# A two-layer hybrid transformer step on one core: late expert rows combined by matmul, final norm tile by tile, z kept in chunk order

## The reference, cut to what matters

```python
def moe(h, router_w, router_b, w_gate, w_up, w_down):
    ...
    gates = jnp.sum(jax.nn.one_hot(idx, N_EXPERTS, dtype=jnp.float32) * w[..., None], axis=1)
    a = jnp.einsum("td,edf->tef", h, w_gate)
    u = jnp.einsum("td,edf->tef", h, w_up)
    z = jax.nn.silu(a) * u * gates[:, :, None].astype(h.dtype)
    return jnp.einsum("tef,efd->td", z, w_down)
...
    x = x + gate1 * mixed
    h2 = rmsnorm(x, norm2_g) * (1 + scale2) + shift2
    x = x + gate2 * moe(h2, ...)
...
    y_prompt = rmsnorm(xp, final_norm_g)
    y_sample = rmsnorm(xs, final_norm_g)
```

## Time and profile before

| | us |
|---|---|
| median of 3 runs | 1341.26 |
| lowest, highest | 1334.2, 1343.4 |
| the profiled execution | 1344.76 |
| its span, first to last instruction | 1343.1 |
| PE busy, DVE busy, ACT busy, POOL busy | 1170.7, 525.6, 371.5, 249.6 |
| layer 0's expert loop, from 387.6 to 661.0; PE's granted clock in it | 273, 0.98 |
| layer 1's expert loop, from 1032.5 to 1306.0 | 273 |

### The profile page before, as it was taken

The page is one execution under the profiler, slowest core; times in us unless marked ns, Lnnn a source line. Parts: engine busy times, 40 slices in busy tenths (PEclk is TensorE's granted clock), DMA queues, the critical chain, the costliest instruction groups (busy, mean ns, idle before and its releaser), DMA issues.

```text
span 1343.1 us, 19689 instructions
## 1 busy us (share of the span) xinstructions
PE 1170.7 (87%) x7740; PEld 540.9 (40%) x7740; DVE 525.6 (39%) x1276; ACT 371.5 (28%) x730; POOL 249.6 (19%) x361
## 2 busy tenths in 40 slices
PE   2899899789969999999629989988896999999980
PEld 0555555354423333333225655555443333333320
DVE  1274666733422111111154747575145111111125
ACT  2123344331312222222121424452222222222221
POOL 1221274220020111110020324440202011111000
PEclk9899889789879999999959997996996999999995
DMA  9738321555769999999380312064733999999924
GB/s 364 258 125 124 65 95 67 213 200 226 317 232 379 382 382 389 400 393 377 113 301 0 134 63 83 12 222 167 300 117 149 346 396 390 391 389 384 391 113 161
DMA packets 51488, 322.71 MB, mean 240 GB/s; under 512 B 8329, under 2 KB 8777, under 8 KB 32080
## 3 DMA queue, kind: packets, MB, share of 16 engines
q1 hardware_dynamic: 37552, 286.87, 55.3%
q0 software_dynamic: 12576, 30.03, 8.4%
q10 hardware_dynamic: 1280, 4.72, 0.9%
HBM read 315.53 MB, written 22.73 MB: 252 GB/s over the span
## 4 chain that ended last, share of the span: by engine, by line
PE 74%; DVE 14%; DMA 7%; issue 2%; ACT 2%; SPq 0%; DVEq 0%; POOLq 0%; ACTq 0%
PE ps L1835 38%; PE ps L1476 18%; PE ps L1724 6%; PE ps L1824 3%; DMA ring<-ada_w 3%; DVE attT L1103 3%; DVE dbuf L1082 2%; PE ps L1487 2%; PE ps L1510 2%; PE ps L1647 1%; PE ps L1618 1%; DMA ring<-w_out 1%; DVE small L1208 1%; DVE dbuf L1078 1%; DMA expert_rows<-big,lst 1%
## 5 line engine op out<-in xcount | busy, mean ns | idle before, releaser
L1835 PE MATMUL ps<-ring,dbuf 128*32 128x512 f32 x3072 | 390.2, 598 | 3.0 <-DVE dbuf L1395 1.6
L1835 PE MATMUL ps<-extra,dbuf 128*32 128x512 f32 x1536 | 198.4, 596 | 0.0
L1835 PEld LDWEIGHTS ps<-ring,dbuf 128*32 128x32 f32 x3072 | 108.6, 111 | 212.9 <-issue 207.4
L1476 PE MATMUL ps<-ring,extra 128*128 128x512 f32 (+1 forms) x384 | 149.8, 550 | 0.0
L1476 PE MATMUL ps<-extra,ring 128*128 128x384 f32 (+1 forms) x384 | 127.8, 481 | 7.6 <-ACT extra L763 5.1
L685 POOL DMA_INDIRECT expert_rows<-big,lst x32 | 30.0, 939 | 468.6 <-DVE big L1416 446.5
L1835 PEld LDWEIGHTS ps<-extra,dbuf 128*32 128x32 f32 x1536 | 56.1, 110 | 121.1 <-issue 120.9
L1476 PEld LDWEIGHTS ps<-ring,extra 128*128 128x128 f32 x384 | 74.0, 194 | 69.7 <-issue 66.2
L1476 PEld LDWEIGHTS ps<-extra,ring 128*128 128x128 f32 x384 | 75.7, 207 | 54.8 <-issue 12.7
L1395 DVE COPY dbuf<-ps 128x384 f32<-128x384 f32 x32 | 17.8, 558 | 200.5 <-PE ps L1824 200.4
L1724 PE MATMUL ps<-ring,extra 128*128 128x512 f32 x192 | 87.5, 612 | 7.6 <-DMA ring<-w_out 6.4
(11 more groups left out here) (281 smaller groups left out, 1393.2 us busy)
## 6 DMA issues: line engine op xcount, KB each, us to landing
ring<-moe_w_up SPq DMA_DIRECT2D x30, 2048.0 KB, 14.1
ring<-ada_w SPq DMA_DIRECT2D x24, 2048.0 KB, 8.9
ring<-moe_w_gate SPq DMA_DIRECT2D x24, 2048.0 KB, 14.0
extra<-moe_w_down SPq DMA_DIRECT2D x22, 2048.0 KB, 14.4
ring<-w_in SPq DMA_DIRECT2D x12, 2048.0 KB, 11.6
ring<-moe_w_down SPq DMA_DIRECT2D x10, 2048.0 KB, 18.5
extra<-moe_w_gate SPq DMA_DIRECT2D x8, 2048.0 KB, 14.8
ring<-w_out SPq DMA_DIRECT2D x4, 2048.0 KB, 9.8
```

Of the source, the lines that this page charges most:

```text
L1476: ins = pe.matmul(out, a, b, start=(n == 0), stop=(n == len(pairs) - 1))
L1835: return pe.matmul(p[QT * g:QT * (g + 1), :], a, w, start=start, stop=stop, tile_position=(0, QT * g))
```

## The change

1. **Routing stretch.** Of the four `AHEAD` blocks in layer 0, the first is multiplied between the two halves of the logits, the second behind `hidden_back(2)`, the last two behind the lists (before: two, one and one, with the first two ahead of `hidden_tile(2)`). `modulation` on DVE moves behind the overflow table. SP holds the weights from the fourth expert block on until the first gather has landed. Layer 1 uses the slot order of layer 0.
2. **Overflow.** Its count is published ahead of the lists (`s_nov`); each engine reads it and branches before the expert loop, in both layers. Code of the loop itself is otherwise the same.
3. **Returned rows.** The last two experts (`LATE`) are not scattered. POOL, having zeroed two buffers during expert 4, gathers the rows of the first 14 experts by six indirect DMAs (two for each tile, rows of the last two left at zero), starting when scatter 13 has landed. DVE prepares 0/1 matrices (`late`) from the lists, and PE adds the last two experts' rows by matmul into PSUM (`cm`, 12 matmuls a layer); `completed` on DVE multiplies by the gate and adds. POOL sums the third tile. `expert_rows` is written once at the start from the inputs.
4. **Final norm.** Gain loaded early, one DVE instruction a tile for scale and gain, `normalize` laid between the sums, a store a tile.
5. **z.** ACT reads PSUM in order and writes in chunk order (512 B steps), DVE reads its PSUM part every fourth column; `zb` is contiguous for PE's four transposes.

```diff
@@ engine SP
+            def overflow_weights(l):
+                o_ = ov[l]
+                sp.wait_ge(s_nov, l + 1)
+                n_ov = sp.value_load(ovt[0:1, 0:1], min_val=0, max_val=MAXOV)
+                with sp.If(n_ov > 0):
...
                     elif kind == "expert":
+                        if j == 3:
+                            overflow_weights(l)
+                            sp.wait_ge(d_g[0], 16 * (NE // 2 * l + 1))
...
-            sp.dma_start(y_prompt[0], xn[:, 0, :]).then_inc(d_y, 16)
-            sp.dma_start(y_sample[0].rearrange("(t p) d -> p t d", p=P), xn[:, 1:3, :]).then_inc(d_y, 16)
+            for t in range(NT):
+                sp.wait_ge(s_y, t + 1)
+                sp.dma_start(y_sample[0, (t - 1) * P:t * P] if t else y_prompt[0], xn[:, t, :]).then_inc(d_y, 16)
@@ engine POOL
+                    if e == EXP_PER_BODY:
...
+                        for k in range(2):
+                            step(pool.memset(yr[k], 0.0))
...
+                    if 0 < e <= NE - LATE:
...
+                pool.wait_ge(s_late, l + 1)
                 for t in range(NT):
-                    pool.dma_start(yr[:, t, :, :], yrow[2 * t * P:2 * (t + 1) * P].rearrange("(p k) d -> p k d", k=2)).then_inc(d_yr[t], 16)
+                    for k in range(2):
+                        pool.indirect_dma_start(yr[k][:, t, :], None, yrow, bass.IndirectOffsetOnAxis(yidx[:, NT * k + t:NT * k + t + 1], 0),
+                                                bounds_check=2 * T - 1, oob_is_err=False).then_inc(d_yr[t], 16)
+                if l == L - 1:
+                    pool.dma_start(fin, final_norm_g.partition_broadcast(P)).then_inc(d_fin, 16)
+                pool.wait_ge(d_yr[2], 32 * (l + 1))
+                y = yr[0][:, 2, :]
+                step(pool.tensor_tensor(y, y, yr[1][:, 2, :], ALU.add))
+                step(pool.tensor_tensor(y, y, gate[:, 1, :], ALU.mult))
+                pool.tensor_tensor(x[:, 2, :], x[:, 2, :], y, ALU.add).then_inc(s_sum2, 1)
@@ engine ACT
-                        act.activation(sS[0:CAP], p[0:CAP], ACT.Silu)
-                        release(act, act.activation(sU[2 * QT:CAP], p[CAP:P], ACT.Copy), ("a", l), e)
+                        act.activation(by_chunk(sS)[0:CAP], in_rows(p)[0:CAP], ACT.Silu)
+                        release(act, act.activation(by_chunk(sU)[2 * QT:CAP], in_rows(p)[CAP:P], ACT.Copy), ("a", l), e)
@@ engine DVE, routing
+                p = ready(dve, ("cnt", l))
+                release(dve, dve.tensor_copy(cnt, p[:, 0:NE]), ("cnt", l))
...
+                dve.tensor_copy(ovt[0:1, 0:1], pin[0:1, NE - 1:NE]).then_inc(s_nov, 1)
                 p = ready(dve, ("lst", l))
...
+                step(dve.tensor_tensor(late[0:CAP].rearrange("p j t c -> p (j t) c"), places[0:CAP].unsqueeze(1).broadcast_to([CAP, LATE * NT, P]),
+                                       tokf[0:CAP].rearrange("p j t -> p (j t)").unsqueeze(2).broadcast_to([CAP, LATE * NT, P]), ALU.is_equal))
@@ engine DVE, end of the layer
+                summed(0)
+                expert(NBODY, 0, last=True, next_=False)
+                summed(1)
+                completed(0)
+                completed(1)
+                normalize(2 * l + 2, 0)
+                dve.wait_ge(s_sum2, l + 1)
+                completed(2)
+                normalize(2 * l + 2, 1)
+                normalize(2 * l + 2, 2)
@@ engine PE
-                for blk in AHEAD[l][0:2]:
-                    mod_rows(*blk)
                 hidden_tile(2)
...
-                        turn("zt", e - 1, [zb_by_f[0:CAP, f, :] for f in range(FC)])
+                        turn("zt", e - 1, [zb[0:CAP, f * P:(f + 1) * P] for f in range(FC)])
...
+                for t in range(NT):
+                    halves = [begin(pe, ("cm", l, t, b)) for b in range(2)]
+                    for j in range(LATE):
...
+                            ins = pe.matmul(halves[b], late[0:CAP, j, t, :], ybuf[0:CAP, j, b * 512:(b + 1) * 512], start=(j == 0), stop=(j == LATE - 1))
```

More of the change, by code:

```diff
@@ L173, in place_jobs @@
             uses[b] += NE
+        for job in [("cm", l, t, b) for t in range(NT) for b in range(2)]:
+            b = n % MOD_BANK
+            uses[b] += 1
+            place[job] = (b, uses[b])
+            n += 1
     return place
@@ L257, in by_row @@
             return v.rearrange("p (q a k) -> p q k a", q=4, k=KC)
-        yr = carve(big, 0, NT, 2, D)
+        yr = [carve(buf, 0, NT, D) for buf in (big, bbuf)]
+        late = carve(bbuf, NT * D, LATE, NT, P)
+        fin = ring[:, SLOTS - 1, 0:D]
         junk = carve(big, 2 * NT * D, D)
@@ L966, in expert @@
                         release(act, act.activation(ybuf[2 * QT:CAP, (es - 1) % 2, 512:1024], p[CAP:P], ACT.Copy), ("dn0", l), e - 1)
+                o_ = ov[l]
+                act.wait_ge(s_nov, l + 1)
+                n_ov = act.value_load(ovt[0:1, 0:1], min_val=0, max_val=MAXOV)
+                with act.If(n_ov > 0):
+                    with act.Fori(0, n_ov) as r:
+                        act.wait_ge(o_["tensor"], 4 * r + 2)
+                        act.activation(sS[0:CAP], ps[0:CAP, 2, :], ACT.Silu).then_inc(o_["scalar"], 1)
+                        act.wait_ge(o_["stored"], 16 * r + 16)
                 turned_out(0, 0)
@@ L1416, in expert @@
                         release(dve, dve.tensor_tensor(half, half, p[0:2 * QT], ALU.add), ("dn1", l), e - 1)
-                turned_out(0, 0)
-                for e in range(EXP_PER_BODY):
-                    expert(0, e, first=(e == 0))
-                with dve.Fori(1, NBODY - 1) as i:
-                    for e in range(EXP_PER_BODY):
-                        expert(i, e)
-                for e in range(EXP_PER_BODY):
-                    expert(NBODY - 1, e, next_=(e < EXP_PER_BODY - 1))
-                expert(NBODY, 0, last=True, next_=False)
                 o_ = ov[l]
+                dve.wait_ge(s_nov, l + 1)
                 n_ov = dve.value_load(ovt[0:1, 0:1], min_val=0, max_val=MAXOV)
@@ L1924, in _ @@
+                for t in range(NT):
+                    halves = [begin(pe, ("cm", l, t, b)) for b in range(2)]
+                    for j in range(LATE):
+                        if t == 0:
+                            for kind in ("dn0", "dn1"):
+                                moved(pe, (kind, l), NE - LATE + j)
                         for b in range(2):
-                            ins = matmuls(ps[0:CAP, 5 + b, :], [(zTg[:, f, :], wd[:, f, b * 512:(b + 1) * 512]) for f in range(FC)])
-                        ins.then_inc(o_["tensor"], 1)
```

236 lines of the change are left out of this document (136 added, 100 removed).

## The result

The changed kernel takes 1327.4 us (median of 8 runs, 1325.0 to 1334.9) beside 1339.0 for the kernel before on the same chip: ratio 0.9926, 95% interval 0.9905 to 0.9946. That is 11.6 us less, where the forecast had 33.6 on the profiled time and some 28 on the median, and its range, 1299 to 1325, ends where the measured times begin. The profiled execution took 1326.6, its span is 1324.6.

A forecast was written before the change was run, and what follows sets the result against it. The prediction took the loop as bound by PE at full clock; its terms, -12.9 -13.0 -5.9 -1.2 +1.4 -2 = -33.6 on the profiled 1344.76, gave 1311.2, stated as 1311 us, range 1299 to 1325.

The forecast's parts named there:

- End of layer 0 and 1: From the last expert to layer 1's transposes, and to the kernel's end: 12.9 and 13.0 us less.
- Tile 1: three of 1.24: At the layer's end, DVE's three sums of tile 1 behind the last expert take 1.24 us each, to 666.2.
- hidden by 6 us: At the layer's end, POOL's sum of tile 2 takes 6.9 us from 661, done at 668, hidden by 6 us.
- Half clock for the combination: Rival at the layer ends: combination tiles take 6.9 us each, gain 3.6 in place of 12.9, total 1330; chance 0.13.
- The six gathers then cost POOL what the gather of layer 1 does: At the end of layer 0, each gather costs POOL 1.04 us to issue, some 0.3 between; one lands after 3.85.
- z: Expert loop: contiguous transposes of zb save 0.1 us in each of 32 experts, weight loads up to 8; taken as -2.
- An expert's period of 16.8 and not over 16.9: Sign in the expert loop: one expert takes 16.8 us and not over 16.9.
- the 2.04 from which they would count: Rival in the loop: ACT's strided copies pace it from 2.04 us each; 1345 and more if 2.6; chance 0.04.
- The held weights: Rival: SP's late fourth block starves the loop, PE waiting in experts 1 to 3, some 8 us, 1319; chance 0.06.
- Routing, layer 0: Routing stretch of layer 0: gate matmuls at 381.7 in place of 387.60, -5.9; their fuller clock another -1.2.
- Routing, layer 1: Routing stretch of layer 1: DVE's added instructions and a load make the copy 1.4 us later (0.7 to 3).
- the rival of loads and branches: Ahead of the loop, register loads and taken branches cost 3 us more in each layer, total 1317; chance 0.11.

The follow-up runs named there:

- e6: The changed kernel with all sums of rows on DVE, tile 1's ahead of the last expert, none on POOL: 1329.3 us, ratio 0.9925.
- e8: The kernel before with six more gathers of hidden rows by POOL behind expert 13's scatter, into unread buffers, both layers: 1345.9 us, one run.
- e9: The kernel before with six plain loads of 96 hidden rows in place of the gathers of e8: 1339.6 us, one run.
- e11: e10 with plain loads of the returned rows in place of the six gathers, each layer with its own zero-filled rows: 1316.6 us, ratio 0.9838.
- e2: The changed kernel with z strided as in the kernel before: 1329.6 us, ratio 0.9933.
- e3: The changed kernel with SP issuing expert blocks before routing, without its share of the overflow path (not a whole kernel): 1318.5 us, ratio 0.9852.
- e4: The changed kernel with SP waiting for layer 0's last expert before issuing the first block of w_in: 1329.2 us, ratio 0.9941.
- e1: The kernel before with only the gate and up parts (z) in chunk order: 1336.4 us beside 1337.9, ratio 0.9993.
- e10: e6 with blocks 3 to 5 issued ahead of routing and loaded a second time if experts overflow; a whole kernel: 1325.2 us, ratio 0.9869.
- e5: The changed kernel without SP's wait for the first gather, still waiting for the overflow count: 1329.3 us, ratio 0.9920.

## Why the prediction failed, step by step

- **End of layer 0 and 1** (-12.9 and -13.0): right in kind, 10.6 and 11.5 measured. The step that failed is "Tile 1: three of 1.24". DVE took 1.67, 3.25 and 1.23 for them, in layer 1 3.24, 1.23 and 1.22, while POOL added tile 2: 2.4 and 2.0 us more than forecast. I had counted POOL's sum as hidden by 6 us; it was off the path, but slowed DVE. The Trainium skill, page SBUF — State Buffer, section SBUF: two separate sides, says that DVE and GpSimd share a pair of ports by an exclusive lock, and that a DVE instruction with two SBUF inputs and a GpSimd one that reads SBUF wait for each other. The trace agrees: 3.25 beside POOL's 3.21, 1.22 without it (e6). The instructions that read PSUM kept their 0.69. Half clock for the combination, the likeliest rival, cost nothing: 24 instructions took 10.54 us in layer 0 and 12.26 in layer 1 for 10.4 at full clock, and DVE did not wait for them.
- **The last experts.** No step had them change. The window row of the changed kernel (busy time by engine, then granted clock, DMA share, GB/s):

```profile
648.00:652.00 4.00, 3.20 (x22) 1.11 (x26) 3.75 (x4) 0.49 (x1) 0.00 (x0) 0.74 0.62 238
```

  "The six gathers then cost POOL what the gather of layer 1 does" priced the gathers on POOL alone; they cost PE 2.7 and 2.8 us at the two ends, and behind PE's idle time the granted clock fell (0.74 in this row), 1.7 us on the last 48 matmuls of layer 0. e8, e9 and e11 show the delay. The fall of the clock is not so firm: behind such idle times, 2.5 to 3.7 us, the 48 matmuls took 6.8 to 8.2 us thirteen times and 5.39 three times (e2, e3, e4).
- **z** (-2): the term was too small on PE, 0.17 per expert and not 0.1, and wrong in the sum: "the loop is bound by PE at full clock" overlooked that the DMA share was 1.00 too (the row in e1). e1 gives 0. "An expert's period of 16.8 and not over 16.9" held, 16.73, until the weights ran out. PE's weight loads for z went from 212 to 141 ns. ACT's strided copies stayed under the 2.04 from which they would count, as said.
- **The held weights** (a rival, 0.06): the mechanism that cost most was named and looked for at the wrong place. I let the supply run short in experts 1 to 3, near the late issue. It ran short from the ninth expert on, where the lead lost at routing and the growth of the lag add up. e3: 9 us, without SP's share of overflow; e10, a whole kernel: 4 to 7.5 below e6.
- **Routing, layer 0** (-5.9 and -1.2): the gather went out 18.1 us behind tile 2's transposes (forecast 18.9) and took about 4 to land, as forecast. PE started the transposes of the rows at once, 23.1 us behind tile 2's (at 371.45), where I had modulation and a load ahead of it for 26.0: two blocks took 3.64 and were done before the rows came. But the results reached DVE at 376.6 and ACT at 378.1: late as in the tail. The first 64 gate instructions took 9.56, so nothing came of the 1.2 for the clock either. Measured -3.8 between the two profiles; kernels with the old order took 31.5, 31.5, 34.9 and 35.2, so at most 1 or 2 us are the change's. I had read the one profile of before as if it had no spread.
- **Routing, layer 1** (+1.4): +1.7 between the two profiles; 24.5 to 24.7 in the kernels with the old code, 26.1 to 27.0 in those with the new but e5: right. The load and the branch are in it: between DVE's last new instruction and its first copy lie 0.9 us in layer 1 (1017.44 to 1018.35), while on PE only 0.3 showed in layer 0 (371.17 to 371.45). So the rival of loads and branches took nothing beyond the sum.
- **The base.** The sum stood on a profile whose first stretch was the longest of fourteen.
- **The range.** Its lower end takes 2.1 for the two blocks, where the sum's own bounds, 5.9 and 7.1, leave 1.2 (and 5.5 less 4 would be 1.5). That moves the end that was not met.

The misses add up: loops 12.5 us, ends 3.9, routing with the clock of its first matmuls 3.6, against 5 us of luck in the first stretch, 15 of the 33.6.

## What to carry over

When an engine is busy through a loop and the DMA share is 1.00 as well, read the time from issue to landing at the loop's start and at its end: if it grows, the lead is a budget, an engine time saved there is given back, and a block issued later ahead of the loop is paid for at its far end. Work moved to an idle engine is not free because it is off the path: ask which port, queue or semaphore it shares with the engine that is on it. And before a stretch of 35 us gets a term of 6, see how much it differs between two runs of the same code.

## What the runs showed of the hardware

- Six gathers by POOL, one behind the other at the end of a layer, made PE's results reach ACT and DVE 0.8 to 4.9 us late (e8: 4.1 and 4.9); six plain loads from the same queue did not (e9). One gather per expert in the loop did not either, and two gathers and six scatters ahead of the loop went with late results in layer 0 of the changed kernel (0.8 to 5.7) and not in e1 (0.01).
- Two-input SBUF instructions of DVE stretched from 1.22 to 3.25 us beside POOL's tensor instruction (e6 without it).
- A gather issued among three weight blocks of 2 MB landed after 11 us in place of 4 (e5).
- ACT's copy out of PSUM, read in order and written in steps of 512 B, took 1.08 to 1.11 us for 0.59; DVE's sum with one strided PSUM input took 0.68 as before.
